# RWKV scan: half of direction 1's 64x64 products moved to the two off-diagonal quadrants of the array

## The reference, cut to what matters

```
def step(s, inp):                      # s: 64x64 per head
    rt, wt, kt, vt, at, bt = inp
    sa = einsum('bhij,bhj->bhi', s, at)
    s = s * wt[..., None, :] + sa[..., None] * bt[..., None, :] + vt[..., None] * kt[..., None, :]
    y = einsum('bhij,bhj->bhi', s, rt)
    return s, y
```

## Time and profile before

| | |
|---|---|
| median of 3 runs | 3681.42 us (3680.19 to 3684.13) |
| span of the profiled execution | 3676.6 us |
| PE busy in the span | 3407.3 us (93%) |
| the scan stage | from about 1509 to 2250 us of the span |
| scan stage, PE busy | 705.57 of 741 us, 20930 matmul records, granted clock 0.99 |
| scan stage, DVE and ACT busy | 507.45 and 366.04 us |
| one round of three n in the steady stretch | 90.67 us |

### The profile page before, as it was taken

How to read it: one execution, slowest core, us unless ns; L and a number is a source line. 1 busy time by engine, 2 the same in 40 slices (tenths; PEclk the granted TensorE clock), 3 DMA queues, 4 the chain that set the end, 5 groups by cost and what they waited for, 6 DMA issues and landing times.

```text
span 3676.6 us, 79518 instructions
## 1 busy us (share of the span) xinstructions
PE 3407.3 (93%) x35550; PEld 2653.0 (72%) x35550; DVE 1631.8 (44%) x3121; ACT 1158.3 (32%) x2449; POOL 400.1 (11%) x616
## 2 busy tenths in 40 slices
PE   7998998999999699899999997999989898899998
PEld 5767977788888488799999985688868776534333
DVE  3354455423323632467767773443444474312112
ACT  3342233312212333355555442322243332100001
POOL 0000122100000100222333320000011200100000
PEclk9999999999999899999999997899999999799999
DMA  5493153111111110000000002122211122589996
GB/s 192 149 351 107 49 242 115 69 69 69 69 47 69 65 46 24 9 6 6 5 6 5 6 4 100 69 92 92 92 67 47 61 92 107 242 372 414 413 428 292
DMA packets 35237, 437.41 MB, mean 119 GB/s; under 512 B 5025, under 2 KB 5633, under 8 KB 9169
## 3 DMA queue, kind: packets, MB, share of 16 engines
q1 hardware_dynamic: 29664, 413.44, 28.1%
q0 software_dynamic: 5232, 18.89, 1.6%
HBM read 425.49 MB, written 6.82 MB: 118 GB/s over the span
## 4 chain that ended last, share of the span: by engine, by line
PE 82%; DMA 7%; DVE 6%; ACT 4%; issue 1%; POOL 0%; SPq 0%; DVEq 0%; ACTq 0%; POOLq 0%
PE ps L755 23%; PE ps L2050 8%; PE ps L2051 8%; PE ps L2052 8%; PE ps L2468 7%; PE ps L3825 6%; DMA part<-in_wu 4%; PE ps L2461 3%; PE ps L2475 2%; PE ps L1010 1%; PE ps L2583 1%; PE ps L2574 1%; PE ps L1327 1%; PE ps L3705 1%; PE ps L2304 1%
## 5 line engine op out<-in xcount | busy, mean ns | idle before, releaser
L755 PE MATMUL ps<-part 128*128 128x256 f32 (+1 forms) x4848 | 876.3, 343 | 43.1 <-DVE part L995 16.9
L755 PEld LDWEIGHTS ps<-part 128*128 128x128 f32 x4848 | 754.9, 193 | 161.3 <-issue 19.1
L2050 PE MATMUL ps<-part 128*128 128x512 f32 (+1 forms) x1536 | 549.8, 358 | 18.1 <-DVE part L2097 11.4
L2051 PE MATMUL ps<-part 128*128 128x512 f32 (+1 forms) x1536 | 549.0, 357 | 0.0
L2052 PE MATMUL ps<-part 128*128 128x512 f32 (+1 forms) x1536 | 548.8, 357 | 0.0
L3825 PE MATMUL ps<-part 128*64 128x512 f32 x1536 | 375.5, 609 | 26.0 <-DMA part<-in_wg 10.3
L2074 DVE TENSOR_TENSOR part<-part 128x1024 fp32r<-128x1024 f32 x128 | 158.4, 1237 | 494.0 <-ACT part L2063 494.0
L2468 PE MATMUL ps<-part 64*64 64x64 f32 x9984 | 341.6, 219 | 11.0 <-DVE part L2619 4.6
L2468 PEld LDWEIGHTS ps<-part 64*64 64x64 f32 x9984 | 316.1, 135 | 32.8 <-DVE part L2721 7.2
L2050 PEld LDWEIGHTS ps<-part 128*128 128x128 f32 x1536 | 290.4, 189 | 67.5 <-DVE part L2097 12.6
L2051 PEld LDWEIGHTS ps<-part 128*128 128x128 f32 x1536 | 290.6, 189 | 46.0
(11 more groups left out here) (418 smaller groups left out, 4339.0 us busy)
## 6 DMA issues: line engine op xcount, KB each, us to landing
part<-in_ada_w SPq DMA_DIRECT2D x36, 2048.0 KB, 9.6
part<-in_mlp_w SPq DMA_DIRECT2D x32, 2048.0 KB, 7.5
part<-in_wg SPq DMA_DIRECT2D x32, 2048.0 KB, 14.5
part<-in_wu SPq DMA_DIRECT2D x32, 2048.0 KB, 12.8
part<-in_wd SPq DMA_DIRECT2D x32, 2048.0 KB, 13.8
part<-in_b_in SPq DMA_DIRECT2D x8, 2048.0 KB, 7.6
part<-in_ab_w_in SPq DMA_DIRECT2D x7, 2048.0 KB, 8.3
part<-in_rkv SPq DMA_DIRECT2D x6, 2048.0 KB, 7.4
```

Source lines behind the costliest of these rows:

```text
L755: mm = pe.e.matmul(ps[:, j * n:j * n + n], lhs, rhs, start=k == ks[0] and i == 0, stop=k == ks[-1] and i == 2)
L2050: pe.e.matmul(ps, wh[:, k, :], hi[:, k, x0:x1], start=k == 0, stop=False)
L2051: pe.e.matmul(ps, wh[:, k, :], lo[:, k, x0:x1], start=False, stop=False)
```

## The change

Some of the products of both directions are put together in one block of instructions, at the place where direction 1's stood, alternating between the directions: per chunk g, direction 0's two heads, then direction 1's two heads. For these, direction 1 gets the half of its output (or of its operands) swapped, `half(hd ^ side)` with side = 1, so its products run on (rows 0-63, columns 64-127) and (rows 64-127, columns 0-63). Because a swapped output has the heads in the other halves, the next product swaps them back: `gram` swaps in and PX swaps out, X turned and XM follow, `rh` swaps out and `uu` swaps back; `y` is swapped out and put back by ACT in two copies of 64 partitions each.

Interleaved this way: `gram` (T0), X turned (T6), PX (T6, T8), XM (T7, T9), `rh`, `uu`, `y`. Each such block waits for what both directions need before its first product. Not interleaved, still on the diagonal: squares, X adds, the second block of T7 (now `XMT`), ka, br, bk, `zz`. In T7, direction 1's XM lies swapped and its second block does not, so the latter gets a bank of its own ("XMT"), and DVE adds direction 1's in two instructions of 256 columns where it was one of 512. Direction 0 keeps its one add of 512 columns, which waits for XMT too. The wait events are as in the diff:

```diff
+    def both_grams(x, two):
+        ends = {}
+        for it in range(2):
+            for j in range(2):
+                for u, out in two:
+                    lhs, rhs = (u.bb, u.aa) if x == 0 else (u.aa, u.bb)
+                    for hd, o in halves():
+                        t = u.toks[it][j]
+                        ends[u.d] = pe.e.matmul(out[half(hd ^ u.side), 2 * it + j, x, :], lhs[o, t], rhs[o, t], start=True,
+                                                stop=True)
+        return ends
+    def both_blocks(*two):
+        ends = []
+        for g in range(4):
+            for ps, to, lhs, rhs, at in two:
+                for hd in range(2):
+                    o = half(hd ^ at)
+                    mm = pe.e.matmul(ps[half(hd ^ to), g * 64:g * 64 + 64], lhs[o, g, :], rhs[o, g, :], start=True, stop=True)
+                    if g == 3 and hd:
+                        ends.append(mm)
+        return ends
-            if turn == 0:
-                pe.wait_ge(K.at("made", *u.key))
-                ...
+            if turn == 0 and u.d:
+                two = []
+                for w in (u.other(), u):
+                    pe.wait_ge(K.at("made", *w.key))
+                    two.append((w, K.bank("gram", *w.key).rearrange("p (g x c) -> p g x c", g=4, x=2)))
+                both_grams(1, two)
+                for d, mm in both_grams(0, two).items():
+                    mm.then_inc(*pe.up(("gram", d, u.n)))
+            if turn in (6, 8) and u.d:
+                lev, two = turn // 2 - 2, []
+                for w in (u.other(), u):
+                    pe.wait_ge(K.at("X", *w.key, lev + 2), K.at("Pf", *w.key))
+                    two.append((K.bank(("PX", lev), *w.key), 0, w.s.Pf, w.XX[:, 0, :, :], w.side))
+                for d, mm in enumerate(both_blocks(*two)):
+                    mm.then_inc(*pe.up((("PX", lev), d, u.n)))
+            if turn in (7, 9) and u.d:
+                lev, two = (turn - 5) // 2, []
+                for w in (u.other(), u):
+                    pe.wait_ge(K.at("M", *w.key, lev), K.at("XT", *w.key) if lev == 1 else {})
+                    two.append((K.bank(("XM", lev), *w.key), w.side, w.XX[:, 1, :, :], w.s.M, 0))
+                for d, mm in enumerate(both_blocks(*two)):
+                    mm.then_inc(*pe.up((("XM", lev), d, u.n)))
+                if lev == 1:
+                    blocks(two[0][0], 256, two[0][3], two[0][2]).then_inc(*pe.up(("XMT", 0, u.n)))
+                    blocks(K.bank("XMT", *u.key), 0, M, XX[:, 1, :, :]).then_inc(*pe.up(("XMT", *u.key)))
+            if part == 1:
+                out = [K.bank("uu", *c) for w, s, g, cs, x, c in both]
+                for w, s, g, cs, x, c in both:
+                    pe.wait_ge(K.at("rh in", *c), K.at("X", *w.key, 5))
...
+                if lev == 1 and u.side:
+                    w = XX[:, 1, :, :].rearrange("p g c -> p (g c)")
+                    v.wait_ge(K.at("XMT", *u.key))
+                    v.e.tensor_tensor(w, w, K.ps.of("XMT", *u.key)[:, 0:256], ADD).then_inc(
+                        *v.up(("X", *u.key, lev + 3), free("XMT", *u.key)))
+                if u.side:
+                    for hd, o in halves():
+                        s.e.activation(t.yb[o, x * 64:x * 64 + 64], K.ps.of("y", *c)[half(1 - hd), 0:64], ACT.Copy).then_inc(
+                            *s.up(("y in", *u.key), free("y", *c)))
```

More of the change, by code:

```diff
@@ L2404, in __init__ @@
         self.wm = s.wm[self.m % 2]
+        self.side = d
         self.c1 = slice(self.m, self.m + 1)
@@ L2407, in __init__, with other @@
         self.kk = K.rw.kk[self.m % 2][:, self.lo:self.hi]
+    def other(self):
+        return Unit(self.K, 1 - self.d, self.n)
     def chunk(self, sub):
@@ L2476, in turned, with both_turned @@
         return mm
+    def both_turned(*two):
+        ends = []
+        for g in range(4):
+            for ps, x, at in two:
+                for hd, h in halves():
+                    o = half(hd ^ at)
+                    mm = pe.e.matmul(ps[h, g * 64:g * 64 + 64], x[o, g, :], K.ident[o, o], start=True, stop=True)
+                    if g == 3 and hd:
+                        ends.append(mm)
+        return ends
     for what, turn, u in rw_turns(K):
@@ L2526, in rw_pe @@
                 blocks(ps, 256, NP[:, 0, :, :], NP[:, 1, :, :]).then_inc(*pe.up((("squares", lev), *u.key)))
[L2527 to L2540, removed]
+            if turn == 6 and u.d:
+                two = []
+                for w in (u.other(), u):
+                    pe.wait_ge(K.at("X", *w.key, 3))
+                    two.append((K.bank("X turned", *w.key), w.XX[:, 0, :, :], w.side))
+                for d, mm in enumerate(both_turned(*two)):
+                    mm.then_inc(*pe.up(("X turned", d, u.n)))
@@ L2541, in rw_pe @@
                 if lev == 1:
[L2542 to L2545, removed]
+                    blocks(two[0][0], 256, two[0][3], two[0][2]).then_inc(*pe.up(("XMT", 0, u.n)))
+                    blocks(K.bank("XMT", *u.key), 0, M, XX[:, 1, :, :]).then_inc(*pe.up(("XMT", *u.key)))
+        if what == "stream" and u.d:
             sub, part = divmod(turn, 3)
-            g, cs, x, c = u.chunk(sub)
-            vm = K.rw.V[u.m % 2][:, x, :]
+            both = [(w, w.s, *w.chunk(sub)) for w in (u.other(), u)]
@@ L2556, in rw_pe @@
                     for hd, o in halves():
[L2557 to L2560, removed]
+                        mm = pe.e.matmul(ps[half(hd ^ w.side), 0:64], w.A[o, g, 0, :], values(w, x)[o, :], start=first,
+                                         stop=True, skip_group_check=True)
@@ L2561, in rw_pe @@
+                    mm.then_inc(*pe.up(("rh", *c)))
             if part == 1:
[L2562 to L2566, removed]
-            if part == 2:
[L2568 to L2576, removed]
-                if u.lat:
[L2578 to L2584, removed]
@@ new lines, in rw_pe @@
+                out = [K.bank("uu", *c) for w, s, g, cs, x, c in both]
+                for w, s, g, cs, x, c in both:
+                    pe.wait_ge(K.at("rh in", *c), K.at("X", *w.key, 5))
+                for (w, s, g, cs, x, c), ps in zip(both, out):
+                    for hd, o in halves():
+                        at = half(hd ^ w.side)
+                        mm = pe.e.matmul(ps[o, 0:64], w.XX[at, 0, g, :], s.RH[at, :], start=True, stop=True)
+                    mm.then_inc(*pe.up(("uu", *c)))
```

54 lines of the change are left out of this document (41 added, 13 removed).

## The result

The changed kernel takes 3709.6 us (median, 3697.3 to 3711.8) where the kernel before takes 3682.8 in the same session: ratio 1.0062, 95% interval 1.0041 to 1.0082. It is 27 us slower; the forecast was 17 us faster. The profiled execution is the longest of the four (3711.8, span 3710.0 us).

The account below looks back on a forecast made before the run. PE was taken to bound the scan with nearly no free time, DVE second with some 10 us free per n. Gains of 2.1 us a round, 17 us over eight rounds, gave 3681.4 - 17 = 3664.4 us; range 3646 to 3712.

Parts of the forecast that it names:

- Pace: PE's interleaved blocks: four quadrants run in parallel, so a paired record takes 14.5 ns of a block instead of 29.
- The ceiling: Scan, PE's interleaved products: 9152 records saving 14.5 ns each, at most 133 us, 16.6 us a round.
- Rival 1: Paired records on PE: pace common to all quadrants; above 18.3 ns slower by over 0.2%, 3689 to 3759 us; chance 0.14.
- The rule of some 25 ns between starts: PE product starts: the skill's minimum of about 25 ns would make the ceiling 37 us and the kernel 3733 us.
- All of T6 to T9's 160 paired records win nothing; they lose 0.81: T4 to T10 of the first n: joint waits make it 13.49 us against 12.68 before.
- 0.06 us back: Joints T6 to T9: PE starts 0.06 us after the DVE instruction it waited for ends.
- each round's 2.1: Scan, a round of three n: gains 0.41 + 0.49 + 1.21 = 2.1 us, eight rounds 17 us.
- uu, "starts at 3.36": First n, T0 to T2: after gram, masks and ACT copies, uu starts at 3.36 us instead of 3.50.
- The clock (rival 4): Scan: PE's standing lowers the granted clock, up to 8 us per 10 us stretch; outweighs the gain, slower; chance 0.04.
- the costs set at nothing: Direction 1's y as two ACT copies, 14 us in all, is hidden; bank order costs nothing.
- the place of the waits: PE waits about 1 us (0.7 to 1.3) before the blocks of T6, T7, T8 and T9, released by DVE.
- rival 5: Joints: more of them are worse than replayed, by over 1 us per n; slower, up to 3710 us; chance 0.05.

Follow-up runs that it names:

- the bursts: Changed kernel with extra gram records ahead of the gram at n = 6, 9 and 12; at n = 6, 576 interleaved records took 15.4 us.
- long_pair: alone_off with gram interleaved, plus 2048 extra gram records of both directions interleaved over four quadrants at n = 6: 3707.1 us.
- one_wait: Changed kernel with both directions' waits before interleaved gram, T6 to T9, rh and uu blocks put together, one per semaphore, DVE's last: 3696.7 us.
- alone_off: Changed kernel with nothing interleaved, direction 1 still on swapped quadrants, T6 to T9 waits put together: 3645.3 us, ratio 0.9901 against the kernel before.
- only_t6to9: Changed kernel with gram, rh, uu and y not interleaved (still swapped), T6 to T9 interleaved with separate waits: 3693.6 us.
- diag_order: alone_off with direction 1 also on the diagonal quadrants, nothing interleaved: 3681.8 us, ratio 0.9999 against the kernel before.
- the long stretches: Four kernels: alone_off with gram interleaved, plus 2048 extra gram records at n = 6 in different quadrant orders or widths: 3703.7 to 3710.4 us.
- the burst of n = 12: Changed kernel with 256 extra gram records at n = 12, blocks of 32 per direction in turn: 320 records took 9.1 us.

## Why the prediction was wrong

**Pace: right, and too short a view.** The paired record was taken at 14.5 ns; it is 14.8. The ceiling, 9152 records at that saving, 133 us, was not there to be had. It assumed that such a pace can be kept up. In the bursts and in long_pair PE ran 128 records at that pace and then stood until the next packet of instructions. Rival 1 asked for a limit to each record, and there is none; the limit lies in the mean over 128. The sum held no term for it: 13.1 us of stalls in 600 us of the change.

**The rule of some 25 ns between starts** ("TensorE: Matmul & The Clock Gate" in the Trainium skill, "Wait — 56ns, not 53.3ns?"), by which I had a forecast of 3733, is not borne out for products on different quadrants: 14.8 ns on average.

**"All of T6 to T9's 160 paired records win nothing; they lose 0.81": this step failed in size.** In the n followed:

| | forecast | measured |
|---|---|---|
| T0 to uu | 3.36 | 3.38 |
| T0 to T4, less than before | 0.75 | 0.91 |
| T4 to T6 | 5.05 | 5.33 |
| T6 to T7 | 2.55 | 2.95 |
| T7 to T8 | 2.78 | 2.90 |
| T8 to rh of T9 | 2.83 | 2.87 |
| T4 to T10 | 13.49 | 14.30 |

The chain was the right one (M, X add, split add, in that order), and each joint is longer than its sum. T4 to T10 loses 1.62 us against before, twice the forecast. A part is the constant "0.06 us back": it is 0.15 to 0.27 where a second direction's waits stand behind the late one, and one_wait, which puts them together, is 12.9 us faster. Another is DVE's prep work. Between the two M of T6 the replay had one piece and 0.79 us from M to M, as in the earlier trace rows; after, the piece takes longer and they are 1.01 apart (DVE after):

```profile
1884.92 0.42 DVE L2779 TENSOR_TENSOR part<-ps,part 128x256 f32<-128x256 f32 x1 [0.42 <-PE ps L2496]
1885.26 0.64 DVE L2726 SCALAR_TENSOR_TENSOR part<-part 128x256 f32<-128x256 f32 x1
1885.93 0.42 DVE L2779 TENSOR_TENSOR part<-ps,part 128x256 f32<-128x256 f32 x1
```

The piece is the same instruction as L2661 before, where it took 0.41. In the trace of the change it takes 0.41 to 0.42 us in the 19 of its 48 executions that meet no GpSimd instruction, and 0.62 to 0.72 in the 29 that do; in this n one is at work:

```profile
1884.89 0.73 POOL L3005 TENSOR_TENSOR part<-part 128x256 f32<-128x256 f32 x1
```

**What the parts make.** Three n without a stall over 0.5 us, one of each kind (n = 11, 9 and 16), take 29.93, 26.74 and 33.77 us. Such a round makes 90.4 us, where it was 90.7 before and 88.6 in the forecast. So without stalls the change would have won next to nothing, and 1.9 us of each round's 2.1 went in the joints: 15 us in eight rounds. The six rounds from n = 4 to n = 21 took 557.1 us, 14.4 more than six such rounds; they hold 12.0 us of stalls. The rest of the miss lies at the two ends of the scan. From its first product to the gram of n = 4 the change takes 11.3 us longer than before (140.0 against 128.7), and from the gram of n = 22 to its last product 5.6 longer (83.9 against 78.3). These two stretches hold 5.3 us of stalls; before had none there. Together, 15 of joints, 13 more than before in the six rounds and 17 at the ends are the miss of some 44 us (27 slower instead of 17 faster).

**uu, "starts at 3.36", was right.** PE's wait for ACT in front of it grew to 16.3 us from 2.1, but the 3.36 has it in it: in 13 of the 22 n after the first, uu starts 3.31 to 3.39 us after the gram. In the nine others it starts at 3.66 to 4.54, and seven of these nine hold a stall over 0.5 us ahead of it.

**The clock (rival 4)** took a part. In the window from 1509 to 1620 us, the start of the scan, the granted clock is 0.85 after where it is 0.95 before (line of after):

```profile
1509.00:1620.00 111.00, 81.10 (x2382) 73.24 (x2384) 65.96 (x176) 48.38 (x134) 32.33 (x64) 0.85 0.04 9
```

From the first product of the scan to its last, the clock is at 1.2 GHz for 64 us after and for 20 before; 33 and 14 of these lie ahead of the gram of n = 4, 24 and 7 behind that of n = 22. With PE busy for some 75% of these stretches, 44 us more at half speed cost up to some 16 us, an estimate from these numbers. That is nearly as much as is lost at the two ends. The prediction expected a clock of 1.00 and gave this rival 0.04. That the joints' idle time lowers it fits only_t6to9's 0.89 in the same window, but one_wait with the same joints has 0.91 and alone_off without them 0.92, and it was not tried by itself.

**The base of the comparison was wrong too.** The prediction let blocks of one direction run strictly one after the other and gave overlap to interleaved ones only. alone_off shows that swapping the quadrants alone gives 36.5 us against diag_order (3681.8 - 3645.3). Interleaving then buys a faster pace that the supply takes back, and pays for it with joint waits. Right in the prediction were the pace, the costs set at nothing, the place of the waits (0.65 to 1.51 us before T6 to T9), and rival 5's mechanism, which it gave a chance of only 0.05. PE was busy for 80% of the scan (616 of 770 us), less than the 85 to 90% expected. That 3709.6 still lies inside the wide range, up to 3712, is luck: the range reached there for rival 1, a slow pace of the paired record, which did not come true.

## What to carry to other kernels

Put neighbouring blocks of independent small products on different quadrants and leave their order alone: their ends overlap by themselves, and nobody waits for the other. Before counting on a faster pace, count instructions: with 64x64x64 products two quadrants already use what the supply brings, so only more work per instruction (here 128 columns instead of 64) makes four quadrants worth having over a long stretch. Where two producers must be waited for together, put the waits on one semaphore into one and the late one last.

## What the runs showed of the hardware that was not expected

- PE's instructions come in packets of 16 KB, 256 instructions, on average 3.6 to 3.8 us apart in the long stretches. A paired stretch runs 128 records in 1.87 us and then stands 1.4 to 1.65 us.
- Products on different quadrants do not start strictly in the order of the program: the first products of the next block start among the last six or so records of the block before (alone_off). One change of quadrants saved 0.17 us in the burst of n = 12.
- Where a second direction's waits stood behind the late one, PE was back 0.146 us (median) and up to 0.35 us after DVE's end; with one wait per semaphore and the late one last, 0.055 us.
- In the change the same DVE instruction on 128x256 (L2726) took 0.41 us alone and 0.62 to 0.72 us with GpSimd at work beside it. In before seven of its executions beside GpSimd took 0.42 us all the same, so not every GpSimd instruction does this.
